# Expert blocks staggered by one on TensorE, down weights' transfers begun by ScalarE, plain row writes, and two projections moved ahead of the first chunk

## What is computed

```python
n = rms_norm(h)
proj = n @ w_in                      # 6160 columns: short conv parts, gate z, SSD parts, dt
y = concat(y_conv, y_ssd)            # convolutions, a chunked state space scan, group norms
h = h + y @ w_out
n = rms_norm(h)
gates, experts = softmax(top_k(n @ router_w + router_b, 4))
for each token and each of its 4 experts e:
    gu  = n @ w_gate_up[e] + b_gate_up[e]
    glu = min(gu[:1024], 7);  lin = clip(gu[1024:], -7, 7)
    h  += gate * ((glu * sigmoid(1.702 * glu) * (lin + 1)) @ w_down[e] + b_down[e])
out = rms_norm(h)[16:]
```

## Time and profile before

| | us |
|---|---|
| median of 3 runs | 1588.57 |
| the profiled execution's own time | 1590.0 |
| its span, first to last instruction | 1588.4 |
| PE busy / DVE busy / ACT busy / POOL busy | 1500.9 / 607.6 / 286.3 / 385.3 |
| data moved | 478.92 MB, 302 GB/s over the span |

### The profile page before, as it was taken

One profiled execution on the slowest core, in us unless ns is written; L12 is line 12 of the kernel. 1 busy time (PEld: TensorE's weight loads), 2 busy tenths in 40 slices (PEclk: granted clock), 3 DMA queues, 4 the chain that ended last, 5 costly groups with the idle time before them and its releaser, 6 DMA issues.

```text
span 1588.4 us, 50367 instructions
## 1 busy us (share of the span) xinstructions
PE 1500.9 (94%) x21338; PEld 964.9 (61%) x21338; DVE 607.6 (38%) x1321; ACT 286.3 (18%) x437; POOL 385.3 (24%) x513
## 2 busy tenths in 40 slices
PE   8998999999994899999999999999999999999995
PEld 6997888875452455555555555555555555555552
DVE  5766889864034223322232223223232232322323
ACT  3533333351021011110111101111011110111102
POOL 2000000000012232433333233232332323323232
PEclk9998999999996899999999999999999999999996
DMA  4221222424454799999999999999999999999994
GB/s 143 85 104 57 106 106 106 158 84 165 162 173 143 279 402 397 408 406 400 403 406 407 400 403 407 406 407 398 405 406 406 404 396 405 404 404 402 398 358 152
DMA packets 88843, 478.92 MB, mean 302 GB/s; under 512 B 16374, under 2 KB 29242, under 8 KB 34674
## 3 DMA queue, kind: packets, MB, share of 16 engines
q1 hardware_dynamic: 65330, 457.03, 71.2%
q0 software_dynamic: 23488, 21.55, 6.8%
HBM read 463.73 MB, written 19.10 MB: 304 GB/s over the span
## 4 chain that ended last, share of the span: by engine, by line
DMA 32%; PE 27%; SPq 6%; issue 1%; DVE 1%; POOL 0%; ACT 0%; POOLq 0%; ACTq 0%; DVEq 0%
DMA ring<-in_moe 32%; PE bank L1470 27%; SPq L421 6%; DMA expert_sum<-moe_f,idx_now 0%; DMA ring<-expert_sum 0%; DMA moe_f<-n_scratch,idx_next 0%; DVE reg_x L1186 0%; DVE reg_b L1174 0%; DVE reg_b L1186 0%; DVE reg_x L1174 0%; POOL slot_table L505 0%; POOL expert_sum L539 0%; DMA idx_raw<-slot_table 0%; POOL idx_raw L519 0%; SPq L339 0%
## 5 line engine op out<-in xcount | busy, mean ns | idle before, releaser
L1470 PE MATMUL bank<-ring,moe_f 128*32 128x256 f32 x18432 | 1012.6, 380 | 35.9 <-DMA ring<-in_moe 24.0
L1470 PEld LDWEIGHTS bank<-ring,moe_f 128*32 128x32 f32 x18432 | 585.5, 110 | 463.0 <-DMA ring<-in_moe 49.7
L1146 DVE STREAM_TRANSPOSE moe_f<-bank 128x384 f32<-128x384 f32 x64 | 37.3, 583 | 649.0 <-PE bank L1470 649.0
L539 POOL DMA_INDIRECT expert_sum<-moe_f,idx_now x96 | 154.2, 1606 | 332.9 <-ACT moe_f L760 302.1
L1199 PE MATMUL bank<-n_hi,w_hi 128*128 128x258 f32 (+2 forms) x608 | 189.0, 311 | 0.2 <-DVE reg_tq L978 0.2
L1199 PE MATMUL bank<-n_lo,w_hi 128*128 128x258 f32 (+2 forms) x608 | 186.7, 307 | 0.0
L1199 PE MATMUL bank<-n_hi,w_lo 128*128 128x258 f32 (+2 forms) x608 | 186.4, 307 | 0.0
L755 ACT ACTIVATE moe_f<-moe_f 128x384 f32<-128x384 f32 x64 | 33.5, 523 | 651.5 <-DVE moe_f L1149 651.5
L532 POOL DMA_INDIRECT moe_f<-n_scratch,idx_next x99 | 104.1, 1052 | 63.1 <-issue 62.3
L1199 PEld LDWEIGHTS bank<-n_hi,w_hi 128*128 128x128 f32 x608 | 114.8, 189 | 7.6 <-issue 1.5
L1199 PEld LDWEIGHTS bank<-n_lo,w_hi 128*128 128x128 f32 x608 | 114.8, 189 | 5.7 <-issue 0.5
...
## 6 DMA issues: line engine op xcount, KB each, us to landing
ring<-in_moe SPq DMA_DIRECT2D x384, 1024.0 KB, 28.9
...
```

The lines of the kernel that those rows point to most:

```text
L539: g.indirect_dma_start(out=acc_parts, in_=y_sb[:, n, :], in_offset=None, out_offset=bass.IndirectOffsetOnAxis(ap=idx_now[:, 2 * n:2 * n + ...
L1146: v.transpose(glu.rearrange("p b (g r) -> p g b r", g=GRANULES), gate).then_inc(gate_raw, 1)
L1470: ins = mm(out[l * LANE:(l + 1) * LANE, g * QUARTER:(g + 1) * QUARTER], x[:, at, g * LANE:(g + 1) * LANE], w[:, l * QUARTER:(l + 1) * QUAR ...
```

## The change

1. PE runs gate and up of block j ahead of down of block j-1 (`gate_up(j)`, `down(j - 1)`). Gate and up accumulate in three PSUM banks with matmuls of 512 columns, 96 per block instead of 192 of 256, and the activation is made in one piece of 768 columns.
2. The 4 down pieces of an expert are no longer begun by SP but by ACT, in its own queue, right behind the eviction of y of the block before. SP begins the 8 others.
3. The rows of y are written plainly, without the gate, each to a row of its own (`expert_rows`, 4 x 512 rows). Slots without a token have an index out of bounds. The table holds the destination in place of the gate. GpSimd gathers three blocks ahead, and keeps the indices of the blocks in between.
4. At the end 8 MB of such rows are loaded in 8 transfers in place of 2 MB in 4; PE adds the first two rows of each token by matmuls with diagonal matrices of gates (16 of 512 columns), DVE the other two. The copy of h to DRAM ahead of the experts is gone.
5. In the first part, projections 0 and 1 of chunk 0 are put ahead of the work on the learned tokens and of the chunk's transposes. The low parts of the first two tiles are made by DVE, not by GpSimd, and the order of the first two tiles' matmuls is changed to suit; one more warming matmul stands before them.

```diff
-            def pieces(j, e):
-                for q in range(PIECES):
-                    hold(piece_used, j * PIECES + (q + 1 - PIECES))
+            def gate_up(j, e):
+
+                for q in range(GU):
+                    hold(gu_used, j * GU + (q + 1 - GU))
                     sp.dma_start(slot(q), moe_d[ds(e, 1), q].rearrange("o p w -> (o p) w")).then_inc(w_in[q], 16)
 
-            with sp.Fori(1, EXPERTS) as j:
-                pieces(j, j)
+            for q in range(GU):
+                hold(gu_used, q + 1)
+                sp.dma_start(slot(q), moe_d[1, q]).then_inc(w_in[q], 16)
+            with sp.Fori(2, EXPERTS) as j:
+                gate_up(j, j)
...
-                sp.dma_start(acc[:, m, :], acc_d[m * P:(m + 1) * P, :]).then_inc(acc_in[m], 16)
+                rows = yk_d.rearrange("(k t) d -> t k d", k=TOPK)[m * P:(m + 1) * P]
+                for hf in range(2):
+                    sp.dma_start(yk(m)[:, 2 * hf:2 * hf + 2, :], rows[:, 2 * hf:2 * hf + 2, :]).then_inc(yk_in[hf][m], 16)
...
-            for t in range(2):
-                pool.wait_ge(wh_ready, t + 1)
-                g.tensor_tensor(w_lo[:, t, :], slot(t)[:, 0:KC * P], w_hi[:, t, :].bitcast(F32), ALU.subtract
-                                ).then_inc(wl_first, 1)
...
             def scatter():
                 for n in range(GRANULES):
-                    g.indirect_dma_start(out=acc_parts, in_=y_sb[:, n, :], in_offset=None,
+                    g.indirect_dma_start(out=yk_parts, in_=y_sb[:, n, :], in_offset=None,
                                          out_offset=bass.IndirectOffsetOnAxis(
-                                             ap=idx_now[:, 2 * n:2 * n + 1].bitcast(U32), axis=0),
-                                         bounds_check=(SEQ + SPARE) * LANES - 1, oob_is_err=True, compute_op=ALU.add
-                                         ).then_inc(y_out, 16)
-
+                                             ap=idx_now[:, 2 * n + 1:2 * n + 2].bitcast(U32), axis=0),
+                                         bounds_check=TOPK * SEQ * LANES - 1, oob_is_err=False).then_inc(y_out, 16)
...
+            with pool.Fori(0, n_blocks - 1) as j:
+
+                hold((xT_ready, j + 3))
                 gather()
-                base = pool.value_load(blocks[0:1, ds(2 * j + 4, 1)], min_val=0, max_val=EXPERTS * CAPACITY - BLOCK)
+                base = pool.value_load(blocks[0:1, ds(2 * j + 8, 1)], min_val=0, max_val=EXPERTS * CAPACITY - BLOCK)
                 list_rows(base)
 
                 hold((y_ready, j + 2))
                 scatter()
-                hold((idx_in, j * (16 * LANES) + 48 * LANES), (x_in, j * (16 * GRANULES) + 32 * GRANULES),
+                hold((idx_in, j * (16 * LANES) + 80 * LANES), (x_in, j * (16 * GRANULES) + 64 * GRANULES),
                      (y_out, j * (16 * GRANULES) + 16 * GRANULES))
-                keep_rows()
+                pool.sem_inc(y_room, 1)
+                move_rows(idx_now, mid1)
                 hold((idx_moved, j * 4 + 8))
-                pool.sem_inc(y_room, 1)
-                lane_rows()
+                move_rows(mid1, mid2)
+                hold((idx_moved, j * 4 + 9))
+                move_rows(mid2, idx_next)
                 hold((idx_moved, j * 4 + 10))
+                lane_rows().then_inc(idx_moved, 1)
+                hold((idx_moved, j * 4 + 11))
+            hold((y_ready, n_blocks + 1))
+            scatter()
...
+            def sigmoid(j):
+                act.wait_ge(glu_ready, j + 1)
+                a.activation(sig, glu, ACT.Sigmoid, scale=ALPHA).then_inc(sig_ready, 1)
+
+            def evict(j):
+                act.wait_ge(dn_used, j * DN + 3 * DN)
                 act.wait_ge(y_room, j + 1)
                 y = bank[:, 4:6, :].rearrange("p a b -> p (a b)")
-                for n in range(GRANULES):
-                    ins = a.activation(y_sb[:, n, :], y[:, n * QUARTER:(n + 1) * QUARTER], ACT.Copy,
-                                       scale=idx_now[:, 2 * n + 1:2 * n + 2].bitcast(F32))
-                ins.then_inc(y_ready, 1)
+                a.copy(y_sb.rearrange("p g x -> p (g x)"), y[:, 0:GRANULES * QUARTER]).then_inc(y_ready, 1)
+
+            sigmoid(0)
+            with act.Fori(1, n_blocks) as j:
+                sigmoid(j)
+                evict(j - 1)
+                e = act.value_load(blocks[0:1, ds(2 * j + 1, 1)], min_val=0, max_val=EXPERTS - 1)
+                for q in range(GU, PIECES):
+                    act.dma_start(slot(q), moe_d[ds(e, 1), q].rearrange("o p w -> (o p) w")).then_inc(w_in[q], 16)
+
+            evict(n_blocks - 1)
...
                 x_transposed(j + 2)
+                dve.wait_ge(gu_free, j + 2)
+                for b in range(FF_BLOCKS):
+                    ins = v.tensor_scalar(up[:, b, :], up[:, b, :], bias_col(1, b), 1.0 - LIMIT, ALU.add, ALU.max)
+                ins.then_inc(up_ready, 1)
+                dve.wait_ge(up_ready, j + 1)
+                dve.wait_ge(glu_ready, j + 1)
+                v.scalar_tensor_tensor(up, up, 1.0 + LIMIT, glu, ALU.min, ALU.mult).then_inc(lin_ready, 1)
+                dve.wait_ge(lin_ready, j + 1)
+                dve.wait_ge(sig_ready, j + 1)
+                dve.wait_ge(dn_used, j * DN + 2 * DN)
+                v.tensor_tensor(act_t, up, sig, ALU.mult).then_inc(act_ready, 1)
...
+                dve.wait_ge(yk_in[1][m], 16)
+                acc = h2[:, m, :]
+                for k in range(2, TOPK):
+                    steps.done(v.scalar_tensor_tensor(o_sb[m], yk(m)[:, k, :], gates[:, m * TOPK + k:m * TOPK + k + 1], acc,
+                                                      ALU.mult, ALU.add))
+                    steps.settled()
+                    acc = o_sb[m]
+                dve.wait_ge(part_done, m + 1)
+                b = PART_BANK[m]
+                v.tensor_tensor(o_sb[m], o_sb[m], bank[:, b:b + 2, :].rearrange("p a b -> p (a b)"), ALU.add
...
+            project(0, 0, 2, META - 4, CHALF)
             pe.wait_ge(pk_ready, 1)
             for q, x in enumerate((dt_t, w_t, acs_t)):
...
+            project(0, 1, 2, META - 4, CHALF)
...
+            turn_chunk(0)
+            rest_of_chunk(0)
+            with pe.Fori(1, TT) as i:
+                turn_chunk(i)
+                project(i, 0, 2, META - 4, CHALF)
+                project(i, 1, 2, META - 4, CHALF)
+                rest_of_chunk(i)
...
+            def lanes(first_bank, width, x, at, w, first, last):
+
+                out = bank[:, first_bank:first_bank - (-GRANULES * width // 512), :].rearrange("p a b -> p (a b)")
+                for g in range(GRANULES):
+                    opens = first and g * width % 512 == 0
+                    for l in range(LANES):
+                        ins = mm(out[l * LANE:(l + 1) * LANE, g * width:(g + 1) * width],
+                                 x[:, at, g * LANE:(g + 1) * LANE], w[:, l * width:(l + 1) * width],
+                                 start=opens, stop=last, skip_group_check=True)
+                return ins
+
+            def piece_here(j, q):
+                pe.wait_ge(w_in[q], j * 16 + 16 * (HELD[q] + 1))
+
+            def gate_up(j):
+
+                pe.wait_ge(xT_ready, j + 1)
+                pe.wait_ge(gu_free, j + 1)
+                for q in range(GU):
+                    piece_here(j, q)
+                    lanes(0, 2 * FF_LANE, xT, q, slot(q), q == 0, q == GU - 1).then_inc(gu_used, 1)
+
+            def down(j):
+
+                pe.wait_ge(act_ready, j + 2)
+                pe.wait_ge(y_ready, j + 1)
+                for q in range(GU, PIECES):
+                    piece_here(j, q)
                     for u in range(2):
-                        w = slot(q)[:, u * D:(u + 1) * D]
-                        if q < GU:
-                            h, c = q // 4, q % 4 * 2 + u
-                            ins = lanes(2 * h, xT, c, w, c == 0, c == KC - 1)
-                        else:
-                            h, c = (q - GU) // 2, (q - GU) % 2 * 2 + u
-                            ins = lanes(4, act_h[h], c, w, (h, c) == (0, 0), (h, c) == (1, FF_BLOCKS - 1))
-                    ins.then_inc(piece_used, 1)
-
-                pe.wait_ge(xT_ready, j + 1)
-                pe.wait_ge(gu_free, j * 2 + 1)
-                for q in range(4):
-                    piece(q)
-                pe.wait_ge(gu_free, j * 2 + 2)
-                for q in range(4, GU):
-                    piece(q)
-                pe.wait_ge(y_ready, j + 1)
-                pe.wait_ge(act_ready, j * 2 + 1)
-                piece(8)
-                piece(9)
-                pe.wait_ge(act_ready, j * 2 + 2)
-                piece(10)
-                piece(11)
-
+                        b = 2 * (q - GU) + u
+                        ins = lanes(4, QUARTER, act_t, b, slot(q)[:, u * D:(u + 1) * D], b == 0, b == FF_BLOCKS - 1)
+                    ins.then_inc(dn_used, 1)
+
+            gate_up(0)
+            pe.sem_inc(dn_used, 2 * DN)
```

(12 more changed lines are left out.)

290 lines of the change are left out of this document (133 added, 157 removed).

## The result

The changed kernel takes **1590.67 us** (median of 20 runs, 1588.5 to 1593.31) against 1588.09 for the kernel before: a ratio of 1.0017, 95% interval 1.0011 to 1.0024. That is 2.7 us slower, where I forecast 1573.0.

| part | before | after | difference | forecast |
|---|---|---|---|---|
| start to first expert matmul | 522.8 | 519.5 | -3.3 | -5.5 |
| experts' loop, to PE's last matmul | 1036.5 | 1028.5 | -8.0 | -25.5 |
| tail, to the end of the span | 29.1 | 42.1 | +13.0 | +15.4 |
| span | 1588.4 | 1590.1 | +1.7 | -15.6 |

What follows compares the result with a forecast made beforehand. PE bounds the loop's first stretch, then DMA, at 33.01 us per block against 31.08. Span 1588.4 - 5.5 (first part) - 25.5 (loop) + 15.4 (tail) = 1572.8, forecast 1573.0 us, own range 1564 to 1583.

Steps and rivals of the forecast that it cites:

- Down pieces on ACT's queue: Experts' loop: ACT gets half the engines; the last down piece lands at 25.6 us, wanted at 28.4; cost nothing.
- DMA per block: 31.5: Experts' loop: transfers need 31.5 us per block (31.4 to 32.3) instead of 33.0, as plain rows replace accumulating scatters.
- residual of 0.5: Experts' loop: 0.5 us of a block's 33.01 us on the DMA queues stayed unexplained and was left in.
- PE per block 31.0: Experts' loop: PE's matmuls take 31.0 us per block, from 31.08; at most 0.3 us can go.
- Start of the loop 5: Ahead of gate_up(1): PE waits 5 us once for DVE; 10 us without open transfers then eat half the 21 us lead.
- End of the loop 10: After down(30): the last down pieces begin late and PE's clock falls, 10 us more.
- Rival (a): Scatters: plain rows as dear per packet as accumulating ones, 1.5 us; DMA needs 32.3 per block, 1595 us; chance 0.13.
- Rival (b): Experts' loop: down pieces come late and PE waits every block, 1.6 us each, 1623 us; chance 0.11.
- Rival (c): Scatters: slots without a token are walked all the same, DMA stays at 33.0 per block, 1622 us; chance 0.04.
- Tail: From PE's end to the span's end: 44.5 us instead of 29.1, a loss of 15.4.
- First part: Before the experts: projections fill PE's idle time, 5 us (0 to 9), and the gate's copy on DVE 0.5; gain 5.5.
- The ceiling of 358 GB/s: Loads from HBM: by this limit a block's weights take 35.1 us, giving 1598; the trace disagreed, so no chance.

Runs made afterwards that it cites:

- e3: The kernel before with its scatters writing plain rows instead of accumulating, the sum over a token's experts left out: 1552.04 us, ratio 0.9768.
- e5: The changed kernel with the kernel before's experts' loop, SP beginning all 12 pieces; plain rows, end combination and new first part stay: 1565.44 us, ratio 0.9860.
- e1: The changed kernel, but SP begins the down pieces too, in PE's order of use, each when its slot comes free: 1572.97 us, ratio 0.9902.
- e2: The changed kernel, but ACT begins each down piece when its slot is free, ahead of the eviction of y: 1584.3 us, ratio 0.9973.
- e4: The kernel before with plain rows, the experts' sum left out, and slots without a token out of bounds: 1550.3 us, ratio 0.9767.
- e6: The changed kernel with projections 0 and 1 of chunk 0 back behind the chunk's transposes: 1592.51 us, ratio 1.0028.

## Why the prediction was wrong

**The ladder.** From ratios, in us, each step against the one ahead of it, the first against the kernel before: plain rows in the old loop -36.8 (e3); the combination at the end and the new first part +14.6 (e5); the stagger with one queue +6.7 (e1); the down pieces on a queue of their own +11.3 (e2); their begin behind the eviction +7.0 (the changed kernel). Together +2.8, of 2.7 measured.

- **"Down pieces on ACT's queue ... Margin 2.8 us, cost nothing."** This step failed. I asked only whether the down pieces come in time, and they do. I did not ask what the gate/up pieces lose beside them, though PE wants those first. The cost is 11.3 us (e1 against e2). I also put their share at half; for 4 us it was 64%, and half or less after that, so it is not the share that I had wrong but what it takes from the other queue.
- **"DMA per block: 31.5", and "31.5 against 31.0 then needs some 20 blocks to catch up".** The second failed term. A block takes 31.8 to 31.9 under plain rows in every kernel in which DMA leads. Against the kernel before that is 1.15 us less, where I took 1.5. My residual of 0.5 should have been 0.9: weights run at 426 GB/s only in short stretches. With the lead cut by the order, DMA led for 21 blocks at 0.95 us: 19.9 and not 4. The idle time of the engines, to which I put the lost lead, was 11 us; its first half, which e1 has too, explains most of the 7 us between e1 and e5. The early end of the lead it doesn't explain: e2 fills them in part (2.0 MB more by 860) and keeps its lead only one block longer.
- **PE per block 31.0:** measured 30.96. **Start of the loop 5:** 4.44, right, but I missed the 2.4 us of low clock behind it and the 2.8 in gate_up(0). **End of the loop 10:** 8.4.
- **Rival (a)**, plain rows as dear as accumulating ones, falls: e3 earns 37 us. My reason against it, that the read and add make the price of 94 ns, is not shown, since the plain rows also land in fewer and larger packets. **Rival (b)**, down pieces late, falls in its mechanism; a kindred one, gate/up pieces late because of them, took its place. **Rival (c)**: the rows of slots without a token are not written, but their packets stay, and this turned out to be worth nothing (e4).
- **Tail:** 42.1 us instead of 44.5, right in kind and size: the loads begin 7.1 us after PE's end instead of 8.3, and a tile takes DVE 5.2 us and not 5.65. **First part:** 3.3 instead of 5.5 in this pair of traces, in part luck. The scan's first matmul came 4.8 us sooner (152.27 against 157.10), where I had taken 5, but e4 has it at 152.49 without any of the change. Behind it 1.5 were lost, most of it on GpSimd, where the reads of the first list begin 4.29 us after the last scatter into the table and not 2.96. e6 gives no more than 1.8 in time.
- What I never did was to cost the plain rows alone in the old loop. By my own numbers they would have given 31.5 against 31.08 with 21 us of lead, that is nearly all of 21 x 1.93 = 40 us, and the stagger would have stood there as a pure loss.

**The ceiling of 358 GB/s.** In e5 the weights alone are read at 395 GB/s over 127 us (50.22 MB). The Trainium skill (DMA: Bandwidth & Descriptors, section Bandwidth) states about 358 GB/s as the limit of loads from HBM. No run here agrees; but the same section also gives that figure as a core's part when both cores of a pair stream, and 425 GB/s for a core by itself, and this kernel runs on one core. I had left that condition out. By an estimate from the Trainium skill's price of a small descriptor (same section) the skipped third of the rows, taken as packets of 1 KB, would be worth 0.33 us per block in which DMA leads, some 3 us between e3 and e4. The trace has no such packets of 1 KB, the intervals are too wide to tell, and the gaps where DMA leads are 31.8 to 31.9 in both.
